# Moving the second layer's rotation table from GpSimd to VectorE in a two-layer decoder trunk

## The reference

```python
for l in range(2):
    h = rms_norm(x, norm1_g[l])
    q, k, v, f, u_pool, u_ssm = split(h @ w_in[l])
    att  = forgetting_attention(q, k, v, f + f_bias)   # 8 heads x 64, causal
    pool = multiscale_pool(u_pool)
    ssm  = s5_mixer(u_ssm)          # 16 groups x 64 complex states, a scan over the tokens
    x = x + concat(rms_norm(att), rms_norm(pool), rms_norm(ssm)) @ w_out[l]
    h = rms_norm(x, norm2_g[l])
    # 8 heads, each: scores against 2 x 128 keys, top 16 of 256 sums -> 16 experts of 16384
    x = x + sum over 128 experts e: gate[e] * gelu(h . u_tab[e]) * v_tab[e]
```

## Time and profile before

| | us |
|---|---|
| median of 3 runs | 1551.18 (1550.46 to 1553.49) |
| the profiled execution | 1550.5 |
| its span in the trace | 1548.7 |
| VectorE busy | 1078.5 (70%) |
| TensorE busy | 1048.0 (68%) |
| GpSimd busy | 612.2 (40%) |
| ScalarE busy | 575.9 (37%) |
| DMA | 621.19 MB, mean 401 GB/s |

### The profile page before, as it was taken

The page is one execution under the profiler, slowest core; times in us unless marked ns, Lnnn a source line. Parts: engine busy times, 40 slices in busy tenths (PEclk is TensorE's granted clock), DMA queues, the critical chain, the costliest instruction groups (busy, mean ns, idle before and its releaser), DMA issues. The chain is left out here.

```text
span 1548.7 us, 19445 instructions
## 1 busy us (share of the span) xinstructions
PE 1048.0 (68%) x6790; PEld 530.3 (34%) x6790; DVE 1078.5 (70%) x2485; ACT 575.9 (37%) x1769; POOL 612.2 (40%) x571
## 2 busy tenths in 40 slices
PE   8998547586675566778676666888586546456654
PEld 6685213234342234333343133433253311111111
DVE  8768996646988867564688858565588984445444
ACT  5644423524443442262344432344244432211222
POOL 0035347643443234344243433334244344444541
PEclk9999777797987788889698778879698877876787
DMA  9289997999999999999999999999999999999996
GB/s 388 81 350 421 421 421 311 369 422 421 421 420 420 421 421 421 421 420 422 381 420 421 422 420 422 421 421 421 421 419 421 421 421 422 422 421 421 421 420 275
DMA packets 86354, 621.19 MB, mean 401 GB/s; under 512 B 9968, under 2 KB 10096, under 8 KB 11760
## 3 DMA queue, kind: packets, MB, share of 16 engines
q0 software_dynamic: 73728, 536.90, 83.6%
q1 hardware_dynamic: 12528, 83.05, 13.1%
HBM read 618.87 MB, written 1.05 MB: 400 GB/s over the span
## 5 line engine op out<-in xcount | busy, mean ns | idle before, releaser
L628 POOL DMA_INDIRECT slots<-experts,idx x512 | 583.0, 1139 | 895.8 <-PE psum L1876 723.4
L1476 DVE CUSTOM_DVE_ANT_0 slots<-slots,h 128x1024 f32<-128x1024 f32 x512 | 620.1, 1234 | 392.0 <-DMA slots<-experts,idx 386.1
L1876 PE MATMUL psum<-slots,diag 64*64 64x512 f32 x4088 | 600.1, 737 | 325.9 <-ACT diag L992 322.0
L1876 PEld LDWEIGHTS psum<-slots,diag 64*64 64x64 f32 x4088 | 176.0, 165 | 697.3 <-ACT diag L992 398.9
L976 ACT ACTIVATE ge<-ge 128x4 f32<-128x4 f32 x130 | 26.7, 205 | 438.7 <-DVE ge L1476 437.6
L976 ACT ACT_TABLE_LOAD x55 | 70.6, 1283 | 202.4 <-DVE ge L1476 202.1
L992 ACT ACTIVATE diag<-cst,ge 128x64 f32<-128x64 f32 x511 | 136.6, 337 | 6.6 <-PE psum L1876 2.4
L983 ACT ACTIVATE ge<-ge,gate 128x1 f32<-128x1 f32 x512 | 109.1, 283 | 4.2
L1799 PE MATMUL psum<-hT,ring 128*128 128x128 f32 x480 | 66.1, 304 | 8.9 <-DMA ring<-weights 7.4
L1799 PEld LDWEIGHTS psum<-hT,ring 128*128 128x128 f32 x480 | 64.6, 220 | 10.0 <-issue 8.0
L1799 PE MATMUL psum<-work,ring 128*128 128x128 f32 x512 | 60.1, 276 | 6.7 <-DMA ring<-weights 6.7
(11 more groups left out here) (302 smaller groups left out, 1152.4 us busy)
## 6 DMA issues: line engine op xcount, KB each, us to landing
ring<-weights SPq DMA_DIRECT2D x30, 1152.0 KB, 10.0
ring<-weights SPq DMA_DIRECT2D x26, 1024.0 KB, 9.3
slots<-weights SPq DMA_DIRECT2D x11, 1024.0 KB, 20.5
slots<-experts,idx POOLq DMA_INDIRECT x512, 21.4
ring<-weights SPq DMA_DIRECT2D x2, 1056.0 KB, 9.1
sml<-small SPq DMA_DIRECT2D x2, 652.0 KB, 13.8
slots<-weights SPq DMA_DIRECT2D x1, 1056.0 KB, 7.2
xs<-x SPq DMA_DIRECT2D x2, 512.0 KB, 13.6
```

Of the source, the lines that this page charges most:

```text
L628: pool.indirect_dma_start(out=slot[:, place(E), :], out_offset=None, in_=src, in_offset=bass.IndirectOffsetOnAxis(ap=idx[:, n % 2, e:e + 1 ...
L1476: ins = dve.tensor_tensor_reduce(u, u, h2[:, n % 2, :], 1.0, 0.0, ALU.mult, ALU.add, d[:, i:i + 1])
L1876: ins = pe.matmul(acc[HALF * half:HALF * half + HALF, i, :], diag[rows, d % DIAGS, :], slot[rows, place(E), D + half * 512:D + half * 512 ...
```

## The change

The three pieces of the table move from quads 14 to 16 to quads 19 to 21 and from GpSimd to VectorE, with W[2] as scratch in place of W[1]. GpSimd's list has only gathers left. ScalarE's wait for the table moves from `sq` of step 1 to `rp` of step 1.

```diff
 MIX1 = (("bu",), ("scan",), ("backA",), ("backB",), ("y", "z"), ("glu", "pool"),
-        ("att0", "max0", "nrm0", "tab5"), ("att1", "max1", "nrm1", "mixp", "tab6"), ("att2", "max2", "nrm2", "tab7"),
-        ("att3", "max3", "nrm3"), ("att4", "attg", "sq"), ("merge", "out0"), ("out1", "x1a"),
-        ("out2", "x1p"), ("out3", "x1"), ("h2T",))
+        ("att0", "max0", "nrm0"), ("att1", "max1", "nrm1", "mixp"), ("att2", "max2", "nrm2"),
+        ("att3", "max3", "nrm3"), ("att4", "attg", "sq"), ("merge", "out0", "tab5"), ("out1", "x1a", "tab6"),
+        ("out2", "x1p", "tab7"), ("out3", "x1"), ("h2T",))
...
-            def tab(n, part):
-                l = n // TILES
-                if part == 5:
-                    pool.wait_ge(S["carry_ready"], TILES)
-                    pool.wait_ge(S["y_psum"], TILES)
-                rotate(l, tt, lag, link, W[1], ((1, 2, 4, 8, 16), (32,), (64,))[part - 5])
-                if part == 7:
-                    pool.tensor_copy(done_[:, :], phase[:, 0, 0:SB]).then_inc(S["rot_ready"], 1)
-
-            run(dict(tab=tab), gather, lambda n, quad: None)
+            run(dict(), gather, lambda n, quad: None)
...
             def sq(n, sec=None):
                 if sec is None:
-                    if n == 1:
-                        act.wait_ge(S["rot_ready"], 2)
                     link(sq_sec(n, 1))
...
                 R = turn_of(n, h)
                 act.wait_ge(S["qT_psum"], q_by(R))
+                if n == 1:
+                    act.wait_ge(S["rot_ready"], 2)
...
-                rotate(0, tt, lag, link, W[3], ((1, 2, 4, 8, 16), (32,), (64,))[part])
+                rotate(n // TILES, tt, lag, link, W[2 if n else 3], ((1, 2, 4, 8, 16), (32,), (64,))[part])
                 if part == 2:
                     told(dve.tensor_copy(done_[:, :], phase[:, 0, 0:SB]), "rot_ready")
+
+            def tab(n, part):
+
+                rotate_(n, part - 5)
```

More of the change, by code:

```diff
@@ L1477, in dots @@
                 told(ins, "dots_ready")
-            run(dict(scan_im=scan_im, inverse=inverse, fold=fold, attg=attg, x1p=x1p, x1a=x1a, h2=h2_, power=power, rotate=rotate_, normA=normA, normT=normT, uT=u_out, cum=cum,
+            run(dict(scan_im=scan_im, inverse=inverse, fold=fold, attg=attg, x1p=x1p, x1a=x1a, h2=h2_, power=power, rotate=rotate_, tab=tab, normA=normA, normT=normT, uT=u_out, cum=cum,
                      warm=blank, h2T=h2T, turnback=turnback, bu=bu, scan=scan, backA=back, backB=back_im, y=y_, glu=glu, qkn=qkn, qkT=qkT,
```

## The result

The changed kernel takes 1539.74 us (1538.30 to 1540.55, 4 runs), the kernel before 1550.82 us (4 runs): ratio 0.9925, 95% interval 0.9908 to 0.9942, 11.1 us faster. In a second set of runs it was 1537.82 against 1549.24, ratio 0.9921 (0.9904 to 0.9938), 11.4 us. The profiled execution took 1538.3 us with a span of 1536.5, 12.2 us under the span of before.

A forecast was written before the change was run, and what follows sets the result against it. DMA engines bound the kernel, idle 15.0 us while GpSimd's table held back gathers. 1550.5 - 15.0 + 0 (table on VectorE) = 1535.5, plus 0.7 for the median: 1536.2 us; range 1533.5 to 1542.

The forecast's parts named there:

- the forecast's own spread: Whole kernel: 1533.5 to 1539 us, from hole count, run scatter, contention and 1 or 2 us of remaining hole.
- the TensorE rival: Rows 15 to 18: TensorE becomes the next bound, 6.1 of the 15 us come back, 1542 us; chance 0.10.
- The hole and its owner: 246 to 300 us: DMA engines lack work because GpSimd's table holds back gathers whose slots are free; 15.0 us.
- The cost on VectorE: Quads 19 to 21: the table's 10.9 us hide in VectorE's waits for gathers; 0 taken, 10.9 at most.
- The delays: Behind the table's three parts on VectorE, next dots start 3.4, 0.7 and 1.1 us late, recovered inside their quads.
- The port rule of the Trainium skill: VectorE with two SBUF inputs and GpSimd reading SBUF block each other; strictly read, 1.3 us higher, 1537.5.
- 15.0 us: 246 to 300 us: idle DMA time in three windows against 421 GB/s, 7.2, 2.9 and 4.9 us, all taken as won.
- The second count in the prediction: Expert rows 59 to 76: 17 rows took 57.0 us against 42.3 at 2.49 each, a hole of 14.7 us.
- the gain is taken back at a later wait: Later routing or a deeper dip to 381 GB/s returns the 15 us, 1551 us; chance 0.05.
- The cover of 3.5 us: A late gather is hidden up to 3.5 us: four rows in flight, 10.0 us, less 6.5 from issue to landing.

The follow-up runs named there:

- gps_late: Changed kernel with the table on GpSimd instead of VectorE, still beside quads 19 to 21: 1543.01 us, 5.2 slower than the changed kernel.
- vec_early: Changed kernel with the table on VectorE but back beside quads 14 to 16, scratch W[1], ScalarE's wait back in sq: 1537.80 us.
- before_add_first: Kernel before, with TensorE adding quad 22 ahead of the row's first routing projection: 1548.79 us, ratio 0.9995 (0.9986 to 1.0005).
- five pieces: Kernel before, with GpSimd's table split into five pieces beside quads 14 to 18 instead of three beside 14 to 16: 1540.67 us.
- before: The kernel before the change, unedited, in the first set of runs: 1550.82 us.
- table_x3: Changed kernel with each part of the second layer's table made three times in its place on VectorE: 1542.75 us, 4.9 slower.
- before_again: The kernel before, unedited, run once more for a second profile: 1550.28 us.

## Why the prediction was right, and by how much it missed

1539.74 us is 3.5 us over the forecast of 1536.2 and 0.7 us over the forecast's own spread (1533.5 to 1539). It lies inside the range because the TensorE rival had stretched that to 1542, and that rival did not come: so much of it is luck. The second set, 1537.82, lies inside the spread.

Right by its steps:
- *The hole and its owner.* Row 60's dot was forecast near 258.5 and is at 259.42 behind attention work, row 76 near 298.5 and is at 299.17. All slices from 232 to 310 us read 421. `gps_late` and `vec_early` show that GpSimd's queue makes the hole and the place doesn't.
- *The cost on VectorE, 0 of 10.9 us.* 1538.08 without the table against 1537.82.
- *The delays.* The three parts end inside their quads, at 312.6, 326.3 and 340.6. Against the run without the table the first dot behind each is late by 3.5, 2.3 and 2.9 us (3.4, 0.7 and 1.1 were worked out), and by the third dot nothing is left of it.
- *TensorE's rival.* Its slow row came once more (quad 15, windows at a mean clock of 0.74), its additions starting at 267.1 (267.5 before), and cost nothing; the next three began at 274.8, 286.5 and 294.7, 9.2 us apart in the mean.
- *The port rule of the Trainium skill (SBUF — State Buffer, section Who interferes with whom) against the move.* Beside part 5 on VectorE three gathers took 0.94, 0.94 and 1.05 us to issue: no blocking there. A gather that began 1.0 us before part 5 took 1.79 and one beside part 7 took 1.42, within the 0.93 to 1.99 that gathers of the same trace take with no table near.

The term that was mis-sized is the **15.0 us** of the hole. I counted it as bytes that were missing against 421 GB/s, a mean over 16 engines, and took that for time. The DMA share in the same windows (0.49, 0.89 and 0.85) would have given 12.5 us. Expert rows lag by 13.9 us at row 76, by 12.2 at the end of the first pair of profiles and by 13.8 in the pair with the second profile of before, and the medians give 11.1 and 11.4. A part of the 15.0 may be engines that wait for the slowest of them, as in the dip at 755; no run separates that part. The second count in the prediction, 14.7 by dot products, was the better kind of count: its 42.3 us for 17 rows without a hole were 43.3. The hole is also not the same in each execution: the profile of `before_add_first`, the same code up to there, lags by 10.4 us at row 76 with 11.5 us of idle DMA time. The medians are over such executions, and one profile of before was taken for all.

The rival "the gain is taken back at a later wait" was half right in its sign: the dip near 766 us did deepen, 3.8 to 5.4 us of mean idle time. But it isn't on the path, as shrinking or removing such a dip moved none of three kernels by a measurable amount.

The cover of 3.5 us was taken for a constant. It is counted from four rows in flight, and under part 5 it came out: of 13.8 us without a gather some 3.7 were hidden. Elsewhere more was hidden: 6.6 of 7.8 us behind the last of five pieces, all of 14.4 us in the kernel after with nine or ten rows in flight, and in the run with three tables all of a gap of 10.9 us before a gather at 329.9. This erred to the safe side and moved only the prices of the Trainium skill's port rule and of the TensorE rival.

What stays open: where the 1 to 3 us between rows 96 and 140 go (`before` 13.8 to 12.1, `table_x3` 7.5 to 4.0, `before_again` none), and what sets the pace of the lagging engine. No edit made a kernel measurably faster than the changed one.

## What to carry to other kernels

An in-order queue that feeds the bound resource should carry nothing else; if it must, what counts is each hold against the work in flight when it begins, not the sum of the holds. Price a hole in the units that the next stage waits for (here landed expert rows), not in mean busy share of 16 parallel engines: a dip whose floor is 1/16 can be free. And work moved onto an engine that waits for the bound resource in the very same rows is free until the waits are used up: here 10.9 us cost nothing, and 32.7 us cost 4.9.

## What the runs showed of the hardware

GpSimd's table and VectorE's dot products (two inputs in SBUF) block one another. A dot takes 1.23 us, and beside GpSimd's part 6 and 7 single ones took far longer. First VectorE's timeline in `before_add_first`, then in `gps_late`, then GpSimd's in `before_add_first`, part 7 without its copy:

```profile
273.50 7.17 DVE L1476 CUSTOM_DVE_ANT_0 slots<-slots,h 128x1024 f32<-128x1024 f32 x1 [1.25 <-DMA slots<-experts,idx]
```
```profile
329.15 5.05 DVE L1475 CUSTOM_DVE_ANT_0 slots<-slots,h 128x1024 f32<-128x1024 f32 x1 [3.35 <-DMA slots<-experts,idx]
```
```profile
273.09 2.07 POOL L590 TENSOR_TENSOR work<-rot 128x512 f32<-128x512 f32 x2
275.11 2.05 POOL L590 TENSOR_TENSOR rot<-rot 128x512 f32<-128x512 f32 x2
277.12 2.47 POOL L590 TENSOR_TENSOR rot<-rot,work 128x512 f32<-128x512 f32 x2
```

One dot stood still through all of part 7: it took from 273.50 to 280.67 and ended 1.1 us behind the last of the six instructions. Part 7 with its copy took 7.6 us; in the first profile of before it took 9.0 us, with two dots of 2.2 and 2.3 us beside it. Who waits differs by execution, and the hole with it (10.4 against 13.9 us of lag); that the one makes the other is not shown. The Trainium skill, SBUF — State Buffer, section Who interferes with whom, names this case, two SBUF inputs on VectorE against a GpSimd instruction that reads SBUF, with full blocking of the second to issue. The trace agrees that the blocking is full; the dot, however, waited for six GpSimd instructions in a row, and not for the one that was under way. Moving the table to VectorE took this away as well: the 512 dots took 632.4 us together before and 627.9 after, which is 4.5 of the 5.6 us by which VectorE's busy time rose less than the table's 10.8.
